# Layer 1's gate/up product as seven block products, and plain f32 products in the second half of the pooling mixer

## What is computed

```python
# layer 0: gating MLP beside sliding-window attention;  layer 1: pooling mixer;  then a feed-forward, D_FF = 2816
for layer in range(2):
    xp = rms_norm(hp, g[0])
    mp = ab_mixer(...) if layer == 0 else pool_mixer(xp, hist, pos, c_w, c_scale)
    hp = hp + rms_norm(mp, g[1])
    hp = hp + rms_norm(swiglu(rms_norm(hp, g[2]), ffn_w_in[layer], ffn_w_out[layer]), g[3])

def swiglu(h, w_in, w_out):
    gu = h @ w_in                       # (tokens, 1024) @ (1024, 2 * 2816)
    return (silu(gu[..., :D_FF]) * gu[..., D_FF:]) @ w_out
```

## Time and profile before

| | us |
|---|---|
| median of 3 runs (least, most) | 990.38 (990.16, 990.46) |
| the profiled execution, its own time | 990.5 |
| its span, first to last instruction | 988.6 |
| layer 0: P pass, from the span's start | 182.7 to 252.4 |
| layer 0: `fast_rest` | 252.4 to 425.2 |
| layer 0: down product | 425.2 to 567.1 |
| layer 1: gate/up with the pooling mixer's second half | 567.1 to 846.1 |
| layer 1: down product, half 1 | 846.1 to 915.9 |

### The profile page before, as it was taken

One profiled execution on the slowest core, in us unless ns is written; L12 is line 12 of the kernel. 1 busy time (PEld: TensorE's weight loads), 2 busy tenths in 40 slices (PEclk: granted clock), 3 DMA queues, 4 the chain that ended last, 5 costly groups with the idle time before them and its releaser, 6 DMA issues.

```text
span 988.6 us, 18137 instructions
## 1 busy us (share of the span) xinstructions
PE 970.2 (98%) x7314; PEld 938.8 (95%) x7314; DVE 687.3 (70%) x1024; ACT 539.0 (55%) x979; POOL 49.2 (5%) x57
## 2 busy tenths in 40 slices
PE   7999999899999999999999999999999999999997
PEld 6799899899999999999999999999999999999886
DVE  5487554788799998876599877888755545444643
ACT  5632665666555555466567665775544444444542
POOL 0080220100000000000000000002000000000000
PEclk9999999999999999999999999999999999999999
DMA  8324122556544544357654685666565555556653
GB/s 271 85 69 112 44 65 65 157 166 174 156 128 142 141 134 133 106 164 201 177 167 143 173 213 161 177 174 192 165 175 169 167 160 148 147 165 186 202 171 133
DMA packets 268339, 150.21 MB, mean 152 GB/s; under 512 B 14874, under 2 KB 259458, under 8 KB 268256
## 3 DMA queue, kind: packets, MB, share of 16 engines
q1 hardware_dynamic: 267792, 148.60, 52.0%
q0 software_dynamic: 224, 0.35, 0.1%
q10 hardware_dynamic: 240, 0.10, 0.0%
HBM read 146.45 MB, written 2.58 MB: 151 GB/s over the span
## 4 chain that ended last, share of the span: by engine, by line
PE 92%; DVE 4%; ACT 2%; DMA 1%; issue 1%; ACTq 0%; DVEq 0%
PE ps L746 23%; PE ps L748 22%; PE ps L747 22%; PE ps L1227 6%; PE ps L1229 6%; PE ps L1228 6%; DVE wlo L1959 1%; PE ps L1181 1%; PE ps L1183 1%; PE ps L1182 1%; DMA raw<-in_ffn_w_in_dram 1%; ACT whi L1378 1%; PE ps L996 1%; DMA scale_rows<-in_c_scale_dram 1%; PE ps L940 1%
## 5 line engine op out<-in xcount | busy, mean ns | idle before, releaser
L1959 DVE TENSOR_TENSOR wlo<-raw,whi 128x1024 fp32r<-128x1024 f32 (+3 forms) x278 | 300.4, 1083 | 164.0 <-ACT whi L1378 163.6
L1378 ACT ACTIVATE whi<-raw 128x1024 fp32r<-128x1024 f32 (+3 forms) x278 | 257.5, 930 | 142.2 <-PE ps L748 120.0
L746 PE MATMUL ps<-xhi,whi 128*128 128x256 f32 (+2 forms) x968 | 282.4, 292 | 0.5 <-DVE wlo L1959 0.5
L748 PE MATMUL ps<-xhi,wlo 128*128 128x256 f32 (+2 forms) x968 | 278.2, 287 | 0.0
L747 PE MATMUL ps<-xlo,whi 128*128 128x256 f32 (+2 forms) x896 | 257.6, 287 | 0.0
L746 PEld LDWEIGHTS ps<-xhi,whi 128*128 128x128 f32 x968 | 182.1, 188 | 2.8 <-issue 0.9
L748 PEld LDWEIGHTS ps<-xhi,wlo 128*128 128x128 f32 x968 | 182.0, 188 | 0.0
L747 PEld LDWEIGHTS ps<-xlo,whi 128*128 128x128 f32 x896 | 168.6, 188 | 0.0
L747 PE MATMUL ps<-mlo,whi 128*128 128x256 f32 (+1 forms) x352 | 101.0, 287 | 0.0
L746 PE MATMUL ps<-mhi,whi 128*128 128x288 f32 (+1 forms) x280 | 81.9, 292 | 0.0
L748 PE MATMUL ps<-mhi,wlo 128*128 128x288 f32 (+1 forms) x280 | 81.5, 291 | 0.0
(11 more groups left out here) (294 smaller groups left out, 1981.1 us busy)
## 6 DMA issues: line engine op xcount, KB each, us to landing
raw<-in_ffn_w_in_dram SPq DMA_DIRECT2D x110, 512.0 KB, 4.0
raw<-in_ffn_w_in_dram SPq DMA_DIRECT2D x88, 256.0 KB, 3.4
raw<-in_ffn_w_out_dram SPq DMA_DIRECT2D x48, 384.0 KB, 3.6
raw<-in_ffn_w_out_dram SPq DMA_DIRECT2D x48, 320.0 KB, 3.2
raw<-in_ffn_w_out_dram SPq DMA_DIRECT2D x22, 512.0 KB, 4.4
raw<-in_ab_w_in_dram SPq DMA_DIRECT2D x10, 512.0 KB, 4.8
raw<-in_ab_w_out_dram SPq DMA_DIRECT2D x10, 256.0 KB, 2.9
raw<-in_ab_w_out_dram SPq DMA_DIRECT2D x20, 128.0 KB, 3.3
```

What stands on the lines that cost most here:

```text
L746: pe.matmul(out, wh, xh, start=first, stop=False)
L748: return pe.matmul(out, wl, xh, start=False, stop=last)
L1378: act.activation(whi[:, m % NSPLIT, 0:n], split_source(m), ACT.Copy).then_inc(w_hi, 1)
L1959: dve.tensor_tensor(wlo[:, s, 0:n], split_source(m), whi[:, s, 0:n].bitcast(F32), ALU.subtract)\
```

## The change

1. `FAST` becomes `(0, 1)`: layer 1 too has a P pass of 22 units and `fast_rest` of 22 column blocks. `ffn_in` and its 88 units go.
2. The stages (1, 1) and (2, 1) are set into the 22 slots of that P pass. (2, 1) has pieces at slots 22 to 32, which are issued at the end of the pass. DVE forms the first combined weights and splits them ahead of that; in layer 0 they came behind it.
3. The pooling mixer's second half isn't split: `plain_pool_products` multiplies float32 by float32, 16 matmuls of 304 columns in place of 48. Its two weight tiles have places of their own; one is loaded by SP, one by ACT's queue. `x_low` and `hist_low` of stage (1, 1) go.
4. Places in SBUF are given by hand (`overlay`). In layer 1 the parts of the inner activations of half 1 are split during `fast_rest` up to f = 11, those of half 0 during the down product of half 1. ACT's table for Sqrt is loaded after the down product of half 1, not before.
5. POOL multiplies and stores the last rows right after `power(4)`, and clears two pads.

```diff
-C_AFTER = ((11, 12), (18, 20))
+C_AFTER = (11, 12)
 STAGE = {
...
-    (1, 1): {"sum": 2, "spread": 4, "scale": (4, 5, 7, 8), "fold": 10, "pre": 12, "again": 14, "x": (14, 15, 16, 17),
-             "hist": 9, "rows": (10, 11), "keep": (15, 16),
-             "windows": (20, 23, 24), "ends": (21, 25), "post": (23, 24, 25, 26), "add": (24, 25, 26, 27)},
-    (2, 1): {"sum": 29, "spread": 31, "scale": (31, 32, 34, 35), "fold": 37, "pre": 39, "again": 41,
-             "x": (41, 42, 43, 44)},
+    (1, 1): {"sum": 1, "spread": 3, "scale": (3, 4, 5, 6), "fold": 7, "pre": 7, "again": 9, "x": (9, 9, 10, 11),
+             "hist": 4, "rows": (8, 9), "keep": (9, 10), "c": (11, 12),
+             "windows": (12, 13, 14), "ends": (13, 14), "post": (13, 14, 14, 15), "add": (14, 15, 15, 16)},
+    (2, 1): {"sum": 16, "spread": 18, "scale": (18, 19, 20, 21), "fold": 22, "pre": 22, "again": 23,
+             "x": (23, 24, 25, 26), "s1": (27, 28), "s2": (29, 30), "s34": (31, 32)},
...
-FAST = (0,)
-EARLY = 13
+FAST = (0, 1)
+PLAIN = ()
...
+            def plain_pool_products(j):
+
+                n = TOK - CUT + HIST + 1
+                tile = raw_tile(NRAW - 1) if j else c_tile
+                if j == 0:
+                    pe.wait_ge(w_loaded[NRAW - 1], c_loaded())
+                    pe.wait_ge(hist_hi, 1)
                     pe.wait_ge(rows_kept, 2)
                     pe.wait_ge(r_kept[0], KEPT[2, 1])
                 for e in range(4 * j, 4 * j + 4):
                     g, o = divmod(e, 2)
-                    ring = POOL_RING[b]
+                    ring = POOL_RING[1]
                     if e >= len(ring):
-                        pe.wait_ge(wide_kept[b], e - len(ring) + 1)
-                    pe.wait_ge(x_lo_done[b], 4 + g + 1)
+                        pe.wait_ge(wide_kept[1], e - len(ring) + 1)
+                    pe.wait_ge(x_scaled[1], 4 + g + 1)
...
+                        mm = pe.matmul(flat(ring[e % len(ring)], 0, n), tile[:, w], xf[:, 2 * g + k, CUT:CUT + n],
+                                       start=k == 0, stop=k == 1)
+                    mm.then_inc(pool_done[1], 1)
...
                 for f, m in enumerate(P_PASS[layer]):
-                    pe.wait_ge(w_lo, m + 1)
+                    pe.wait_ge(w_lo, split_no(m))
...
                     elif f == 0:
-                        pe.wait_ge(z_out[0], 6)
-                    elif f == 1:
+                        pe.wait_ge(wide_kept[0] if layer else z_out[0], KC if layer else 6)
...
                     elif f == FC - 3:
-                        run(LAST)
+                        if layer == 0:
+                            run(LAST)
                         first_terms(layer, 0)
                         second_term(layer, 0)
-                        lo_part(AT["ta", layer, 0])
+                        if layer:
+                            last_term(layer, 0)
+                        else:
+                            lo_part(AT["ta", layer, 0])
                     elif f == FC - 2:
-                        last_term(layer, 0)
+                        if layer:
+                            lo_part(AT["ta", layer, 0])
+                        else:
+                            last_term(layer, 0)
+                    elif f == FC - 1 and layer:
+                        lo_part(AT["tb", layer, 0])
+                run(LAST)
...
-            ffn_in(1, 0, stepper(pooling(1)))
-            ffn_in(1, 1, idle)
-            ffn_out(1, 1, idle)
+            fast_first(1, stepper(pooling(1)))
+            fast_rest(1)
+            ffn_out(1, 1, stepper(splits(1)))
```

More of the change, by code:

```diff
@@ L122, in unit_sequence @@
     for layer in range(2):
[L123 to L132, removed]
+        seq += [("p", layer, f) for f in range(FC)]
+        for f in range(FC):
+            seq += [("ta", layer, f)] + [("tc", layer, f - 1)] * (f > 0) + [("tb", layer, f)]
+        seq.append(("tc", layer, FC - 1))
         for b in FO_ORDER[layer]:
@@ L148, with split_no @@
            for layer in range(2) for b in range(2)}
+SPLIT_UNITS = [unit[0] != "p" or unit[1] == 0 or unit[2] not in PLAIN for unit in UNITS]
+def split_no(m):
+    return sum(SPLIT_UNITS[:m + 1])
 def out_bank(layer, b, d):
@@ L166, in split_count @@
 def split_count(layer, b, f):
[L168 to L176, removed]
+    before, early = SPLITS[0] * layer, EARLY[layer]
+    if b != layer:
+        return before + early + len(LATE[layer]) + f // 2 + 1
+    return before + (f + 1 if f < early else early + (f - early) // 2 + 1)
+SPLITS = [early + len(late) + len(PAIRS) for early, late in zip(EARLY, LATE)]
 def z_count(s, d):
@@ L470, in late_hi, with overlay @@
-        def late_hi(f, last):
-            i = f - EARLY
-            return xhi[:, i // 2, CUT * (i % 2):CUT * (i % 2 + last - f)]
-        def inner_parts(layer, b, f):
-            if layer not in FAST:
-                hi, lo = (half_a, half_b)[b]
-                return hi[:, f, :], lo[:, f, :]
-            if b:
[L481 to L487, removed]
+        def overlay(first, *specs):
+            with ExitStack() as scope:
+                if first:
+                    sb(f"room{first}_{specs[0][0]}", [P, first], F32, scope)
+                return [sb(name, shape, dt, scope) for name, shape, dt in specs]
@@ L1235, in fast_rest @@
                 a22 = xhi[:, half:KC, b], xlo[:, half:KC, b]
-                s2, s3 = [(s_hi[:, i, :, :], s_lo[:, i, :, :]) for i in range(2)]
+                s2, s3 = [(s_hi[layer][:, i, :, :], s_lo[layer][:, i, :, :]) for i in range(2)]
                 s4 = xhi[:, 0:half, frames(0)], xlo[:, 0:half, frames(0)]
@@ L1367, in hi_part @@
             def hi_part(m):
+                if not SPLIT_UNITS[m]:
+                    return
                 if UNITS[m][0] == "ta":
@@ L1892, in fast_rest @@
                 gate_other(FC - 1)
-                for step in range(len(LATE)):
-                    if step >= 3:
+                for step in range(len(LATE[layer])):
+                    if step in (3, 4):
                         hi_part(u + step)
```

555 lines of the change are left out of this document (265 added, 290 removed).

## The result

The changed kernel takes 1005.92 us (median of 4 runs, 1004.11 to 1008.23) against 990.42: ratio 1.0158, interval [1.0136, 1.018]. It is slower, as forecast, but by 15.5 us and not by 5. The profiled execution took 1005.22 us. All of the change lies in layer 1's gate/up stage, which grew by 15.2 us.

A forecast was written before the change was run, and what follows sets the result against it. PE's matrix work was taken as the bound. The profiled 990.5, less layer 1's gate/up 279.0, plus a P pass of 110.8 (PE 77.3, waits 32, clock 1.5) and `fast_rest` 172.8, gave 995.1 us; range 987 to 1001.

The forecast's parts named there:

- The gain and `fast_rest`: Layer 1's gate/up: 264 fewer matmuls of 256 columns save 31.4 us of PE; `fast_rest` takes layer 0's 172.8 us.
- The plain f32 products: Mixer's second half in the P pass: 16 products of 304 columns at 0.53 us, 8.5 us (6.2 to 9.0).
- Item 1: P pass, slot 1: PE waits 2.0 us for ACT's copy `p1`, behind ACT's table load.
- Item 2: P pass, slot 9: PE waits 2.7 us for the guard and POOL's two powers, with nothing between.
- Item 3: P pass, slots 13 to 16: PE waits 4.0 us for ACT's copy `p1` of product 15, behind mixer output.
- item 5: P pass, slots 18 to 21: DVE sets the pace; ACT's `p1` of product 21 is late, 1.8 us.
- Item 4: P pass, slot 16: the sums of (2, 1) wait 2.0 us for DVE's last add.
- The clock: Start of `fast_rest`: low clock for its first matmuls after some 20 us near idle, 1.5 us lost (0 to 2.8).
- Its own signs of being wrong: Wrong if the gap before `fast_rest` is under 15 us, ACT's `p1` copies are never late, or `fast_rest` exceeds 175.
- item 6: End of P pass: stage (2, 1) from slot 22 on has no PE work covering it; PE idles 19.6 us.
- The middle of the pass is smooth: Rival, P pass: items 2 to 5 (10.5 us) don't arise; table load, tail and clock stay: 984.6 us; chance 0.19.
- Much slower: Rival, P pass: handovers cost 0.3 us over some 25, or loads come late; P grows by 5: 1000 us; chance 0.16.

The follow-up runs named there:

- e3_fill: Changed kernel plus 116 unneeded identity products on PE in places where it would wait in layer 1's P pass, nothing reordered: 997.10 us, ratio 1.0073.
- e8_keep_fill: Changed kernel with Silu table load later, half 1's pieces and `rows_kept` earlier, and 79 identity products in PE's waits: 985.09 us, ratio 0.9944.
- e2_order: Changed kernel with PE's second sums of squares of stage (1, 1) put ahead of the turned history rows: 998.91 us, ratio 1.0084.

## Why the prediction was wrong in size

- **The gain and `fast_rest`: right.** PE's busy time fell by 19.2 us, and with the 9.6 of the low clock taken off by 28.8, for some 29. `fast_rest` has layer 0's work and took 174.9 us for 172.8, and the 2.1 more is what its low first 4.7 us lost.
- **The plain f32 products: right, by a shaky working.** The two groups of 8 took 4.26 us each, 0.53 a product, as was taken. But the 1.19 us for 544 columns of the earlier trace rows are 0.28 us for 128 columns, and 0.66 for 304, not 0.24 and 0.56; the result bears out the price and not that division.
- **The waits: right in place, cause and sum.** Item 1 was 3.43 for 2.0, since ACT had waited 0.81 and 0.72 us for the loads of two weight tiles before (563.97 and 565.75) and its table load began 1.4 us later than in the earlier trace rows. Item 2 was 3.81 for 2.7: POOL's two powers took 2.60 and 0.84 us, where the earlier trace rows had 0.54 and 1.73. Item 3 was 4.14 for 4.0, item 5 1.79 for 1.8, the tail 18.9 for 19.6. Item 4 was 0.48 for 2.0, as the low clock filled it: with the clock held high, in `e3_fill`, it was 1.72. That the sum came out within 0.5 us is partly luck, as two items were over by 1.1 and 1.4, and two under by 1.5 and 0.7.
- **"The clock": this is the step that failed.** It expected the low level only after the 20 us of the tail, at 1.5 us, and put it at nothing behind items 1 to 5 without giving a reason. The runs show it behind the waits of 3.4 to 4.1 us inside the pass as well, at 9.6 us in all by the count of slow matmuls, 9.3 by what filling gave back in PE's busy time, and 8.8 in the time of `e3_fill`. The term was short by 8.1 us of the 10.1 by which the profiled execution missed 995.1.
- What is left of the 10.1: waits +0.5, PE's own work other than the clock +1.9 (86.7 less 7.5 is 79.2, for 77.3), less 0.55 us by which the pass started earlier. Sums, spreads and transposes were the loosest term there: 79.2 less 62.8 and 8.5 leaves 7.9 for the 6 taken, and no run took them apart.
- **Its own signs of being wrong.** The single wait ahead of `fast_rest` was 14.95 us and so just under its 15, but with the waits for sums and powers the tail idled for 18.9, as item 6 says. `fast_rest` took 174.91 for its limit of 175. None of the signs named was about the clock inside the pass, so none could catch the step that failed.
- **The rivals.** "The middle of the pass is smooth" would have given 984.6. `e8_keep_fill` reached that time, but only with the order changed and the clock held, so the kernel as changed was never near it. "Much slower", at 1000, was nearer in size than the forecast, for another reason than the true one: with handovers at 0.3 us for 0.1 the waits would have summed to some 5 us more than forecast, and they summed to 0.5 more.

The Trainium skill, TensorE: Matmul & The Clock Gate, What's actually happening, says that the low clock is the default and that activity lifts it, which the trace bears out three times in this pass and once behind it: a low level behind idle time, and full speed again after 3 to 9 us of work. The same section puts the cost of the ramp below 1% of a typical span; here four low stretches together cost 9.6 of 1003.4 us, just under 1%, and that was most of the miss.

## What to carry to other kernels

When a cover is shortened, sum the waits that appear, and then price the long ones a second time: in this stage PE ran 3 to 9 us at half clock behind each wait of 2.9 us or more that was not filled. Shorter ones are uncertain. Waits of 1.78, 1.87 and 2.14 us were followed by the low level in one kernel or another, and waits of 1.78, 2.37 and 2.59 were not. Where the wait can't go, products that nothing reads, into a free part of PSUM, give this back (8.8 us here, and 5.8 in the reordered kernel). Moving work forward out of a tail helps only up to where the engine that does it is never idle; look for its idle time first.

## What was not expected of the hardware

- The level fell at different moments: behind the first wait (3.43 us) PE first did a few matmuls at 0.119 us, from 573.3 to 574.3, and only then went to 0.214; behind the second it was low at once. In `e2_order` it was low at once behind the first wait too, at nearly the same length (3.40 us). No run here gives the length of wait from which the clock falls.
- A pair of DVE's two-input operations took three times as long beside a multiply of POOL's. In the kernel after, the two on `xf` at 614.84 took 3.05 us, the first of them 2.62; the same line at 610.79 took 0.94 for two, and POOL's multiply of `last_rows` stood from 614.38 for 2.77:

```profile
610.79 0.94 DVE L2256 SCALAR_TENSOR_TENSOR xf<-h,gains,r_pre 128x288 f32<-128x288 f32 x2
...
614.84 3.05 DVE L2256 SCALAR_TENSOR_TENSOR xf<-h,gains,r_pre 128x288 f32<-128x288 f32 x2
```

The Trainium skill, SBUF — State Buffer, Who interferes with whom, describes this as a port pair that the two engines share and that the later one waits for. The rows agree: DVE's first operation ended at 617.46, 0.3 us after POOL's multiply (617.15). No run isolated it, and it did not hold PE up.
- Why POOL's first power took 2.60 us in place of 0.54 is open; it was not tried.
